# Key and query transposes moved into the last weight piece, prompt mixers made ahead, and the softmax sink as a score column

## The reference, cut to what matters

```python
def latent_attention(q, k, v, k_ctx, v_ctx, sink):
    ...
    p = jax.nn.softmax(jnp.concatenate([s_loc, s_ctx, sk], axis=-1), axis=-1)
    ...
def pool_mixer(p, pool_w, pool_scale):
    ...
        mixed = (mean - pg.astype(jnp.float32)).astype(p.dtype)
        outs.append(mixed @ pool_w[g])
    return jnp.concatenate(outs, axis=-1) * pool_scale
...
        mix = jnp.concatenate([attn, pool_mixer(p, pool_w[l], pool_scale[l])], axis=-1) @ w_out[l]
        xs = xs + g1 * mix
        h = modulate(rmsnorm(xs, norm_ffn[l]), sh2, sc2)
        xs = xs + g2 * expert_choice_ffn(h, w_router[l], w_gate[l], w_up[l], w_down[l])
```

## Time and profile before

| | |
|---|---|
| three runs | 3645.41, 3647.79 (median) and 3655.09 us |
| the profiled execution | 3642.58 us |
| its span | 3640.8 us |
| mean granted TensorE clock | 0.958 of full speed |

### The profile page before, as it was taken

The page is one execution under the profiler, slowest core; times in us unless marked ns, Lnnn a source line. Parts: engine busy times, 40 slices in busy tenths (PEclk is TensorE's granted clock), DMA queues, the critical chain, the costliest instruction groups (busy, mean ns, idle before and its releaser), DMA issues.

```text
span 3640.8 us, 52731 instructions
## 1 busy us (share of the span) xinstructions
PE 3324.1 (91%) x21164; PEld 3018.2 (83%) x21164; DVE 2164.3 (59%) x2374; ACT 1767.1 (49%) x1900; POOL 569.1 (16%) x611
## 2 busy tenths in 40 slices
PE   5899999998799989997859999999999999999991
PEld 4677777777678877886759999999999999999991
DVE  5634334354452245224877777777877777778774
ACT  5543433455462246223335555555555555555552
POOL 1055036101421013103110000000000000000001
PEclk8999999999899989997979999999999999999995
DMA  7764555477314411343657888888888888888876
GB/s 255 257 237 166 173 189 197 159 273 257 112 40 151 161 67 53 120 148 103 208 184 251 273 271 269 266 262 264 255 277 273 270 269 267 259 266 256 276 232 256
DMA packets 544953, 775.89 MB, mean 213 GB/s; under 512 B 16160, under 2 KB 409600, under 8 KB 536144
## 3 DMA queue, kind: packets, MB, share of 16 engines
q1 hardware_dynamic: 507072, 616.60, 51.8%
q0 software_dynamic: 37776, 157.84, 13.6%
HBM read 708.19 MB, written 66.19 MB: 213 GB/s over the span
## 4 chain that ended last, share of the span: by engine, by line
PE 77%; DVE 7%; ACT 5%; issue 4%; DMA 4%; POOL 3%; ACTq 0%; POOLq 0%; DVEq 0%
PE PS L814 30%; PE PS L606 13%; PE PS L816 12%; PE PS L770 10%; PE PS L716 2%; DVE wlo L1170 2%; ACT whi L887 2%; PE PS L696 2%; PE PS L553 1%; PE PS L734 1%; PE PS L554 1%; DVE lo_f L1459 1%; PE PS L704 1%; ACT hi_f L1094 1%; DMA arena_ab<-k_rope 1%
## 5 line engine op out<-in xcount | busy, mean ns | idle before, releaser
L814 PE MATMUL PS<-xT,hi_f 128*128 128x320 f32 x4096 | 1054.9, 346 | 0.0
L1459 DVE TENSOR_TENSOR lo_f<-raw_f,hi_f 128x2048 fp32r<-128x2048 f32 x384 | 878.8, 2289 | 247.7 <-ACT hi_f L1094 247.4
L816 PE MATMUL PS<-xT,lo_f 128*128 128x160 f32 x4096 | 965.8, 236 | 0.0
L1170 DVE TENSOR_TENSOR wlo<-raw,whi 128x2048 fp32r<-128x2048 f32 x204 | 472.1, 2331 | 642.9 <-ACT whi L887 642.4
L816 PEld LDWEIGHTS PS<-xT,lo_f 128*128 128x128 f32 x4096 | 782.2, 191 | 0.0
L1094 ACT ACTIVATE hi_f<-raw_f 128x2048 fp32r<-128x2048 f32 x384 | 733.2, 1909 | 88.3 <-PE PS L816 83.0
L814 PEld LDWEIGHTS PS<-xT,hi_f 128*128 128x128 f32 x4096 | 768.7, 188 | 0.0
L887 ACT ACTIVATE whi<-raw 128x2048 fp32r<-128x2048 f32 x204 | 387.3, 1916 | 534.0 <-PE PS L770 283.1
L814 PE MATMUL PS<-hid,hi_f 128*128 128x320 f32 x2048 | 533.6, 346 | 0.0
L816 PE MATMUL PS<-hid,lo_f 128*128 128x160 f32 x2048 | 482.8, 236 | 0.0
L816 PEld LDWEIGHTS PS<-hid,lo_f 128*128 128x128 f32 x2048 | 390.7, 191 | 0.0
(11 more groups left out here) (267 smaller groups left out, 4692.5 us busy)
## 6 DMA issues: line engine op xcount, KB each, us to landing
raw_f<-w_gate SPq DMA_DIRECT2D x128, 1024.0 KB, 5.5
raw_f<-w_up SPq DMA_DIRECT2D x128, 1024.0 KB, 5.4
raw_f<-w_down SPq DMA_DIRECT2D x128, 1024.0 KB, 5.4
raw<-w_ada SPq DMA_DIRECT2D x96, 1024.0 KB, 5.2
raw<-w_in SPq DMA_DIRECT2D x60, 1024.0 KB, 5.4
raw<-w_out SPq DMA_DIRECT2D x48, 1024.0 KB, 5.1
arena_ab<-x_sample POOLq DMA_DIRECT2D x8, 1024.0 KB, 12.1
arena_cd<-x_sample POOLq DMA_DIRECT2D x8, 1024.0 KB, 6.6
```

Of the source, the lines that this page charges most:

```text
L814: nc.tensor.matmul(PS[:, b + m, 0:2 * CAP], hi_f[:, n % NSPL_F, r, w], x, start=(kt == 0), stop=False, skip_group_check=True)
L816: ins = nc.tensor.matmul(PS[:, b + m, 0:CAP], lo_f[:, n % NSPL_F, r, w], x[:, 0:CAP], start=False, stop=(kt == last_kt), skip_group_check= ...
L1170: nc.vector.tensor_tensor(wlos[slot(n)], raws[slot(n)], whis[slot(n)].bitcast(F32), ALU.subtract).then_inc(lo_ok, 1)
L1459: nc.vector.tensor_tensor(lo_f[:, n % NSPL_F], raw_f[:, n % NRAW_F], hi_f[:, n % NSPL_F].bitcast(F32), ALU.subtract).then_inc(f_lo_ok, 1)
```

## The change

It does five things.

1. PE turns the keys and first queries of chunk 1 and 2 inside the last weight piece of the chunk before, one unit behind each token block (`turn_keys`). DVE copies them out between the blocks' residuals (`copy_keys`).
2. The sink logit is copied by DVE into one more score column before the mask, so that the exp covers 897 columns rather than 896 and its row sum holds the sink. The ACT exp of the sink and the DVE addition go.
3. DVE evicts the low part of an `M` one unit later, behind the next head's mask; ACT evicts the four heads' high part behind the scaling of the row, no longer before it.
4. The two splits at chunk 0's `M1` and `M2` move ahead of attention. For chunks 1 and 2 one is made at the end of the projection before and one at `M1`. The squares and the root of the last column group are made at the projection's end; what is left of the routing is spread over more units.
5. POOL makes all four prompt mixers ahead of chunk 1's residual stores, into the parts of `kT` and `vv` that the prompt doesn't use.

```diff
         def turn_at(tc):
-            return unit_start[tc] + (2 if CH[tc][2] == 0 else 1)
+            return first_unit(tc) + 1
         def route_at(tc):
-            return turn_at(tc) + 2
+            return turn_at(tc) + (3 if CH[tc][2] else 1)
+        def first_unit(tc):
+            return q_unit(tc, 0) + 1 if tc else 0
+        def mixed_rows(tc, gi):
+            if CH[tc][2] and gi < 3:
+                return mix_p[gi], pw_p[gi]
+            return pin[:, :, HALO:HALO + CH[tc][1] * P], pw
...
+                            if final:
+                                last.then_inc(used if m == nt - 1 else out_ok, 1)
+                                k = unit_start[tc + 1] + m if cc == 3 and tc < 2 else n_units
+                                if tc < 2 and k < first_unit(tc + 1):
+                                    if m < 2:
+                                        pe.wait_ge(lg_ok, u)
+                                    else:
+                                        pe.wait_ge(copied, copies_by(k - 1))
+                                    turn_keys(k).then_inc(unit_pe, 1)
...
-                        nc.scalar.activation(sm[:, s, 3:4], sinks[:, 0, h:h + 1], ACT.Exp,
-                                             bias=sm[:, s, 1:2]).then_inc(sank, 1)
...
+                if tc < 2:
+                    split_hi()
+                    squares(4 * tc + 3)
+                    row_root(tc)
...
-                    dve.wait_ge(sank, head[0] + 1)
-                    link(nc.vector.tensor_tensor(s[:, 4:5], s[:, 2:3], s[:, 3:4], ALU.add))
-                    nc.vector.reciprocal(s[:, 5:6], s[:, 4:5]).then_inc(sum_ok, 1)
+                    dve.wait_ge(exped, head[0] + 1)
+                    nc.vector.reciprocal(s[:, 5:6], s[:, 2:3]).then_inc(sum_ok, 1)
...
                             dve.wait_ge(p_tr, through)
+                            nc.vector.tensor_copy(pp[:, s, w:w + 1], sinks[:, 1, h:h + 1])
+                            dve.wait_ge(unit_pe, k + 1)
...
+                if tc < 2:
+                    split_lo()
                 add_logits(4 * tc + 2)
-                residual(4 * tc + 3)
+                for m in range(nt):
+                    residual(4 * tc + 3, m)
+                    if tc < 2 and unit_start[tc + 1] + m < first_unit(tc + 1):
+                        copy_keys(unit_start[tc + 1] + m)
+                if tc < 2:
+                    row_squares(tc)
...
-                        if gi:
+                        if gi and cond == 0:
                             mixer(tc, gi)
...
-                    mixer(tc + 1, 0)
+                    for gi in range(1 if tc == 0 else 4):
+                        mixer(tc + 1, gi)
```

More of the change, by code:

```diff
@@ L680, in _ @@
                         flat = PS[:, pair:pair + 2, :].rearrange("p a b -> p (a b)")
[L681 to L690, removed]
+                        if kd in "KQ":
+                            last = turn_keys(k)
                         elif kd == "H":
@@ L771, in _ @@
                                                         start=(first and z == 0), stop=(final and z == 2))
[L772 to L774 removed]
+                            if final:
[4 more added lines that the diff above has]
+                                        pe.wait_ge(lg_ok, u)
+                                    else:
+                                        pe.wait_ge(copied, copies_by(k - 1))
+                                    turn_keys(k).then_inc(unit_pe, 1)
+                        if place < 3:
+                            last.then_inc(used, 1)
             turn_x1(11)
@@ L1034, in _ @@
                         pair = 2 * (k % 2)
+                        if tc and gi == 1:
+                            split_hi()
                         act.wait_ge(unit_pe, k + 1)
@@ L1048, in _ @@
                                              PS[:, 4, :].rearrange("p (a b) -> p a b", a=4), ACT.Copy).then_inc(pt_a, 1)
-                    head = behind(tc, j, lag_v)
-                    if head and head[1][3] % 4 == 3:
-                        hc, (_, _, b, h) = head
-                        act.wait_ge(pv_ok, hc + 1)
-                        nc.scalar.activation(ahi[:, h - 3:h + 1, b * P:(b + 1) * P],
-                                             PS[:, 6 + h // 4, :].rearrange("p (a b) -> p a b", a=4), ACT.Copy).then_inc(o_hi, 1)
                     head = behind(tc, j, 1 if cond else 0)
@@ L1061, in _ @@
                         nc.scalar.activation(v, v, ACT.Copy, scale=sm[:, s, 5:6]).then_inc(p_ok, 1)
+                    head = behind(tc, j, lag_v)
+                    if head and head[1][3] % 4 == 3:
+                        hc, (_, _, b, h) = head
+                        act.wait_ge(pv_ok, hc + 1)
+                        nc.scalar.activation(ahi[:, h - 3:h + 1, b * P:(b + 1) * P],
+                                             PS[:, 6 + h // 4, :].rearrange("p (a b) -> p a b", a=4), ACT.Copy).then_inc(o_hi, 1)
                 if tc == 2:
@@ L1243, in _ @@
                         normed(ITEMS[j][1] + 1)
+            for _ in range(NOUT):
+                split_lo()
             dve.wait_ge(mod_tr, 1)
@@ L1301, in router_max @@
                 nc.vector.tensor_copy(rs16[:, 0:nt, :], rs2[:, 2, cs].unsqueeze(2).to_broadcast([P, nt, EXT])).then_inc(rs_ok, 1)
+            def router_max(tc):
+                t0, nt, cond = CH[tc]
+                cs = slice(t0, t0 + nt)
+                dve.wait_ge(lg_ok, 4 * tc + 4)
                 a = aff[:, cs, :]
@@ L1386, in _ @@
                                               flat_t[:, c0 * P:(c0 + z1 - z0) * P].rearrange("p (a b) -> p a b", b=P)).then_inc(pt_v, 1)
+                    head = behind(tc, j, 0)
+                    if head and not cond:
+                        share(head)
                     head = behind(tc, j, lag_v)
@@ L1393, in _ @@
                                                 ahi[s].bitcast(F32), ALU.subtract).then_inc(o_lo, 1)
-                    head = behind(tc, j, 0)
-                    if head and not cond:
-                        share(head)
+                    if tc and j == MIX_AT[cond][1][0] * NH + MIX_AT[cond][1][1] + 2:
+                        split_lo()
                 def top_round(c0, c1, k):
```

120 lines of the change are left out of this document (67 added, 53 removed).

## The result

The changed kernel takes 3607.74 us (median of 4 runs, 3599.29 to 3613.36), where the kernel before took 3646.6 us beside it (3639.77 to 3655.09). The ratio is 0.9891, 95% interval [0.9872, 0.9911], a gain of 39 us (32 to 47 by the interval). The prediction was 3613 us, from a sum of 29 us of gain. In the kernels of the experiments they shift by up to two lines more.

A forecast was written before the change was run, and what follows sets the result against it. PE was taken as busiest but not full, losing time where it waits or runs at half clock. Terms 7.9 - 1 + 7 + 8 - 11 + 18 = 29 us off 3642.6 gave 3613.6, stated as 3613; eight in ten, 3592 to 3631.

The forecast's parts named there:

- the forecast's case of 22 to 40: Whole kernel: a gain of 22 to 40 us, given a chance of 0.50.
- Chunk 2, +18: Chunk 2's attention: early mixers, earlier start and moved splits gain 18 us (10 to 24).
- 11 earlier: Chunk 2's start: M1 comes at about 1686, 11 us earlier than the 1697.17 before.
- Chunk 1's start, +8: Piece's end to seventh head's scores: waits 11.9 and half clock 5 go, 9.1 of new costs; gain 8 us (3 to 15).
- Splits ahead of chunk 0, -1: Ahead of chunk 0: splits hidden, but two 1 MB loads may share queues with the router's rows; 1 us lost.
- Chunk 0's M1 and M2, +7.9: Chunk 0: moved splits and later low part remove stalls behind both products; gain 4.0 + 3.9 = 7.9 us.
- Chunk 1's M1 and M2, +7: Chunk 1: the same two stalls mostly go; gain 7 us, of which 9 is the bound.
- Evictions and sink column, -11: Chunks 0 and 1: 16 evictions -11, small transposes +3, held sink copies -3; together 11 us lost (0 to 22).
- The -3: Sink column: DVE's copies at heads that meet a mixer are held while POOL works; 3 us lost.
- the larger gain (3592): Rival: PE's slack covers the evictions' new place and chunk 1 starts clean, gain 47 to 50 us; chance 0.22.
- The small gain: Rival, 3627: short waits pull the clock down at the 16 evictions, leaving a gain of 16 us; chance 0.16.
- the slower case: Rival, 3660: late masks cost up to a head (3.9 us) per eviction; loss from 2.5 us each; chance 0.05.

## Why the prediction was right, term by term

The sum was 29 us against the profiled execution. One execution against one, the profiles show 31.1; by all runs the gain is 39 (32 to 47), inside the forecast's case of 22 to 40, but above its sum. Most signs came (waits of 3.0 gone from chunk 0, no wait for POOL, the seventh head at 40 us, chunk 2 in 56). Two did not: a wait of 3.54 for the score eviction stands in chunk 1, behind a held router step, and no sink copy came near 2 us.

That the sum closed is in part luck. By place, the 31.1 are: ahead of chunk 0 -8.7, chunk 0 +11.1, chunk 1's start +10.8, its rest +2.4, chunk 2 +19.7, the two projections in which the transposes now lie -3.5, and everything behind -0.9. For chunk 0 the terms make 7.9 less half of the 11 for evictions and sink, some 2.4; it gained 11.1. Ahead of it the term was -1, and 8.7 were lost.

- **Chunk 2, +18.** Measured 19.7. The mixers alone are 16. The part "11 earlier" was right in time (M1 at 1674.53, 20.9 us behind the piece's end, for 31.3) and right in its reason for the mixers; keys and queries in the piece give nothing there.
- **Chunk 1's start, +8.** The stretch went from 51.2 to 40.4, less about 3 of transposes inside the piece: 7.8. With the keys behind the piece again it was 44.2, counted the same way (1295.33 to 1339.50), so the keys are 3.8 of it before those 3; the table loads ahead of the first exponential are the likeliest source of the rest, but I did not undo them alone. The new waits were sized well: 1.9 for the query copy (1.93), 2.2 for the low part (1.81), 3 for held router steps (3.54).
- **Splits ahead of chunk 0, -1.** Measured -4.7, beyond the bound of 3: the router's wait is 14.79 with the two 1 MB loads beside its rows and 10.09 without. The other 4.0 of the 8.7 belong to no term: the last matmuls ahead of the wait ended that much later in a part of the program that is the same in both kernels. In the profiles of the kernels changed only behind it, that point varies by over 10 us.
- **Chunk 0's M1 and M2, +7.9.** Putting the splits back costs 5.9; putting the low part back alone costs nothing. So the splits were the larger cause, and the low part's 1.41 ahead of the mask, which the earlier trace rows show in the same chain, costs nothing without them.
- **Chunk 1's M1 and M2, +7.** Not measured alone. The rest of chunk 1 gained 2.4 us (128.2 to 125.8) with the evictions' loss and the sink's gain in it, and the late split brought a wait of 3.28 behind a DVE subtraction that took 3.95 us for 2.29.
- **Evictions and sink column, -11.** The net was near zero. The evictions' new order costs 12 to 16 us (two kernels, one on each engine), where the terms were -11 and +3: the waits of 0.40 to 0.98 us were sized well (0.7 forecast), but each costs 0.28 more than its length, so that the six in chunk 0 make 3.5 us of waits and 5.5 in all. The sink column gives 13 to 14 where I wrote -3. The failed reasoning is "takes an addition and an ACT instruction off a chain that had slack". At the eviction heads the chain has no slack, because the same change took it away. The -3, for copies held by POOL, was nothing: the longest of 80 took 147 ns.

These single undoings make 21 us rather than 39: 15, 13, 3, 0 and 2 by the ratios, less 12 for the order. With 10 to 15 us of noise in each, that is no proof that the rest is something else. Two parts that each remove the same stall could also hide each other when one is undone, and the moved splits and table loads of chunk 1 were not undone. How the gain divides stays open.

Of the rivals, the larger gain (3592) had the right price and the wrong mechanism: it held that PE's slack covers the evictions' new place, and it does not; without those waits the kernel does run at 3592. The small gain's mechanism, that short waits pull the clock down, is refuted: the clock stayed at 1.00, and what each wait costs beyond its length is 0.28 us and not 1.6. No run came near the slower case: at an eviction PE waits 0.40 to 0.98 us, 0.7 to 1.3 with its surcharge, against the 2.5 from which it would decide.

The Trainium skill, "GPSIMD Engine Reference", section "Specifications", makes DVE contend with GpSimd for two SBUF inputs or a two-port mode. The trace agrees for two inputs (1.85 us for 0.15); the fp32 copy of one element was not held in any of 80, so the prediction's reading, that the rule exposes it like the addition, did not come true. No trace shows in which mode an instruction ran. The Trainium skill, "ScalarE: Activation LUTs", section "What ACT_TABLE_LOAD costs", adds a drain to each switch. Here ACT's timeline at chunk 1's start has none (the second load starts at once behind the root, and the exponential behind it waits 0.69 us for DVE), so the sum that went by rows was the right one:

```profile
1294.96 1.28 ACT L1030 ACT_TABLE_LOAD   x1
1296.26 0.21 ACT L1030 ACTIVATE rs<-rs 128x4 f32<-128x4 f32 x1
1296.48 1.28 ACT L1054 ACT_TABLE_LOAD   x1
1298.46 1.05 ACT L1054 ACTIVATE arena_cd<-arena_cd,sm 128x897 f32<-128x897 f32 x1 [0.69 <-DVE sm L1400]
```

## What to carry to other kernels

When a bundle moves the time, undo its parts one at a time: here one part cost 12 to 16 us inside a gain of 39, and only taking it out alone showed it, and moving one subtraction behind the next mask won it back. Slack is a property of a place and not of an engine: ask which instructions of the same change have used it before an operation of 0.28 us is called free. A transfer or wait that is shortened is worth only the distance to the next thing that is late; look it up (here POOL's columns) before counting the gain.

## What was not expected of the hardware

- A DVE operation on 128x1 fp32 took 129 to 147 ns in all 80 executions as a copy, and up to 1854 ns as a maximum of two SBUF inputs, while GpSimd worked. A scaling of 128x4 with one input took 1.79 us.
- Waits of 0.40 to 0.98 us, eight in 137 us, left the granted clock at 1.00, but each cost 0.28 us more than its length (0.68 for 0.40, 0.94 for 0.66). The lower clock stood behind waits of 3.28 and 3.54 us (0.66 granted over 10 us). In the kernel before, it stood behind the wait of 3.01 us at 1002.06 (0.57 from 1000 to 1008) and not behind the next one of the same length at 1043.73, where the row took 1.83 us and 1.00 was granted from 1040 to 1048.
- PE waited 4.7 us longer for the small router rows beside two 1 MB loads on another queue (14.79 and 10.09 us; 13.94 to 14.94 in eleven profiles, 10.09 to 10.19 in three), and POOL's columns took 16.98 and 12.79 us as the same loads moved.
